# Tokens transposed while the modulation weights land, and the state-space heads with running sums kept as rows: one core, a hybrid block with mixture of experts

## The reference, cut to what matters

```python
mod_l = split((silu(c) @ w_ada + b_ada), 6); mod_c = split((silu(c_ctx) @ w_ada + b_ada), 6)
hl = rmsnorm(xl, norm1_g) * (1.0 + scale) + shift          # hc the same for the context
u = h @ w_in                                               # split in GLA | RWKV-7 | state space
...
# state space, 8 heads of 64, forward and backward, chunked
cum = cumsum(a);  decay = exp(where(causal, cum[:, None] - cum[None, :], -inf))
y = (einsum('tn,sn->ts', cm, bm) * decay) @ xdt  +  (cm * exp(cum)) @ s_start
...
kk = k * rw_kk; kk = kk * rsqrt(sum(kk * kk) + 1e-12); k = k * (1 + (a - 1) * rw_ka)
...
x = x + gate * (concat(o1, o2, rmsnorm(y * silu(z))) @ w_out)
x = x + gate2 * moe(rmsnorm(x, norm2_g) * (1 + scale2) + shift2)   # top 4 of 32 experts, d_ff 1024
return rmsnorm(x, final_norm_g)
```

## Time and profile before

| | us |
|---|---|
| median of 3 runs | 1395.98 (1394.66 to 1396.46) |
| profiled execution, span | 1395.1 |
| PE busy | 1289.9 (92%) |
| DVE busy | 377.9 (27%) |
| ACT busy | 250.8 (18%) |
| GpSimd busy | 48.9 (4%) |
| loaded from HBM | 451.8 MB, mean 325 GB/s |

### The profile page before, as it was taken

The page is one execution under the profiler, slowest core; times in us unless marked ns, Lnnn a source line. Parts: engine busy times, 40 slices in busy tenths (PEclk is TensorE's granted clock), DMA queues, the critical chain, the costliest instruction groups (busy, mean ns, idle before and its releaser), DMA issues.

```text
span 1395.1 us, 21339 instructions
## 1 busy us (share of the span) xinstructions
PE 1289.9 (92%) x9112; PEld 602.2 (43%) x9112; DVE 377.9 (27%) x910; ACT 250.8 (18%) x543; POOL 48.9 (4%) x81
## 2 busy tenths in 40 slices
PE   5999999968789999999999999999999999999997
PEld 2555466657678533333333333333333333333333
DVE  0214526855433221112111211121111211121112
ACT  2332212344331310101110111011100111011101
POOL 0002100051100000000000000000000000000000
PEclk9999999979989999999999999999999999999999
DMA  9464430130217699999999999999999999999994
GB/s 392 188 232 160 180 129 1 61 121 4 85 43 308 253 424 426 427 427 428 428 428 427 428 428 428 428 428 428 428 428 427 427 426 427 428 427 428 428 428 172
DMA packets 33482, 453.96 MB, mean 325 GB/s; under 512 B 3744, under 2 KB 4000, under 8 KB 4352
## 3 DMA queue, kind: packets, MB, share of 16 engines
q1 hardware_dynamic: 33408, 452.86, 77.4%
HBM read 451.79 MB, written 1.05 MB: 325 GB/s over the span
## 4 chain that ended last, share of the span: by engine, by line
PE 75%; DMA 12%; DVE 8%; ACT 2%; issue 2%; SPq 0%; DVEq 0%
PE PS L1823 72%; DMA arena<-in_moe_w_gu 10%; DMA arena<-in_ada_first 2%; PE PS L2591 1%; DVE arena L1717 1%; DVE arena L1241 1%; DVE arena L1723 1%; DVE arena L1720 1%; DMA arena<-in_ada_rest 1%; PE PS L2582 1%; DVE arena L1716 1%; PE PS L2241 0%; PE PS L1835 0%; DVE arena L1391 0%; DVE arena L1489 0%
## 5 line engine op out<-in xcount | busy, mean ns | idle before, releaser
L1823 PE MATMUL PS<-arena 128*64 128x512 f32 (+9 forms) x8762 | 1244.1, 425 | 62.1 <-DMA arena<-in_ada_first 15.5
L1823 PEld LDWEIGHTS PS<-arena 64*64 64x64 f32 (+5 forms) x8762 | 563.6, 149 | 688.9 <-issue 592.7
L1716 DVE TENSOR_SCALAR arena<-PS 128x256 f32<-128x256 f32 x64 | 38.6, 603 | 512.6 <-PE PS L1823 512.6
L1082 ACT ACTIVATE arena<-arena 128x256 f32<-128x256 f32 x64 | 26.7, 417 | 486.1 <-DVE arena L1716 486.1
L1745 DVE TENSOR_TENSOR arena<-PS,arena 128x512 f32<-128x512 f32 x32 | 22.1, 692 | 214.1 <-PE PS L1823 214.1
L1092 ACT COPY arena<-PS 128x256 f32<-128x256 f32 x32 | 11.9, 373 | 275.6 <-PE PS L2582 275.6
L2591 PE MATMUL PS<-arena 128*128 128x128 f32 x128 | 26.3, 287 | 32.2 <-DVE arena L1723 32.2
L1073 ACT ACTIVATE arena<-PS,arena 128x128 f32<-128x128 f32 x128 | 48.2, 457 | 36.9 <-PE PS L1823 36.9
L2591 PEld LDWEIGHTS PS<-arena 128*128 128x128 f32 x128 | 14.4, 142 | 58.5 <-DVE arena L1723 42.4
L1717 DVE TENSOR_SCALAR arena<-PS 128x256 f32<-128x256 f32 x64 | 39.2, 612 | 0.0
L1500 DVE COPY arena<-PS 128x384 f32<-128x384 f32 (+2 forms) x48 | 23.1, 488 | 56.4 <-PE PS L1823 56.2
(11 more groups left out here) (247 smaller groups left out, 371.1 us busy)
## 6 DMA issues: line engine op xcount, KB each, us to landing
arena<-in_moe_w_gu SPq DMA_DIRECT2D x128, 2048.0 KB, 25.4
arena<-in_moe_w_down SPq DMA_DIRECT2D x64, 2048.0 KB, 26.7
arena<-in_ada_rest SPq DMA_DIRECT2D x16, 1024.0 KB, 7.6
arena<-in_w_in SPq DMA_DIRECT2D x5, 2048.0 KB, 8.4
arena<-in_ada_first SPq DMA_DIRECT2D x4, 2048.0 KB, 14.4
arena<-in_w_out SPq DMA_DIRECT2D x4, 1024.0 KB, 5.8
arena<-in_tokens SPq DMA_DIRECT2D x1, 2048.0 KB, 20.9
arena<-in_consts SPq DMA_DIRECT2D x1, 1536.0 KB, 31.6
```

The costliest lines, as they stand in the source:

```text
L1082: act.activation(sgm[:, 256 * half:256 * half + 256], glu[:, 256 * half:256 * half + 256], ACT.Sigmoid, scale=ALPHA).then_inc(sig_ready, 1)
L1716: dve.tensor_scalar(by_rest(glu), of_half(0), LIMIT, None, ALU.min).then_inc(glu_ready, 1)
L1823: ins = pe.matmul(out, lhsT, rhs, start=start, stop=stop, skip_group_check=skip)
```

## The change

**Loads.** The tokens go ahead of the modulation weights; `mats` and the remaining constants go behind the first group of w_in and the next modulation block, and that block ahead of the second group.

**Opening.** The tokens are transposed and normalized between the modulation steps (after n = 1, 3 and 5). ScalarE and VectorE copy the pairs h0 to h3 out of PSUM as they are, into a buffer `raw` that lies over space used later. When shift and scale are there, both engines apply them from `raw` to `hT`, five k-blocks by VectorE and three by ScalarE, and the first projection waits for each block by itself. The time steps' matmuls go behind the second projection's first tile. There are fewer `stay_busy` matmuls.

**State-space heads.** The decays' logarithms are stored four times beside each other (`adt4`), so that four matmuls (`cs`) give the running sums of all sixteen as rows; ScalarE copies them to `sum_rows`, and `running_sums(q)` becomes four matmuls that spread a row over all partitions with a column of the identity, the two heads' in row groups 0 and 32, in turn. The time step is multiplied into the inputs by token (`xdt`, four VectorE operations out of PSUM) and not into the weights. Two of the six blocks of a head's weights need no clamp and are exponentiated by ScalarE straight from PSUM with a bias; VectorE clamps four blocks of 128, and multiplies all six with the scores in one operation. `WD` and `CI` hold four heads. `head_pair` alternates between the two heads. GpSimd's share of RWKV's inputs goes to VectorE. All three orders are rewritten.

```diff
+H_BY_VEC, H_BY_ACT = (0, 1, 3, 4, 6), (2, 5, 7)
...
-    t += [("Bt", 3, 1), ("sc", 0, 1), ("rk", 1, 1), ("cc", 3, 1), ("ada2", 4, 1), ("mt2", 4, 1), ("go", 3, 1), ("xst0", 2, 1), ("rr", 0, 1),
+    t += [("Bt", 3, 1), ("sc", 0, 1), ("rk", 1, 1), ("cc", 3, 1), ("cs", 3, 1), ("ada2", 4, 1), ("mt2", 4, 1), ("go", 3, 1), ("xst0", 2, 1), ("rr", 0, 1),
-    t += [("st", 1, 1), ("rv", 0, 1), ("rz0", 1, 1), ("rz1", 1, 1), ("ra", 1, 1), ("rkn", 0, 1), ("rg", 1, 1), ("rvt", 0, 1), ("cr", 1, 1)]
+    t += [("st", 1, 1), ("rv", 0, 1), ("rkn", 3, 1), ("rz0", 1, 1), ("rz1", 1, 1), ("ra", 1, 1), ("rg", 1, 1), ("rvt", 0, 1), ("cr", 1, 1)]
...
-            for n in (0, 2, 4):
+            sp.dma_start(xtok, a["tokens"]).then_inc(x_in, 16)
+            for n in (0, 2, 4, 6):
                 load_ada(n)
-            sp.dma_start(xtok, a["tokens"]).then_inc(x_in, 16)
-            load_ada(6)
...
+            for i in range(4):
+                R.arrived(act, f"h{i}")
+                R.drained(f"h{i}", act.copy(raw[:, 2 * i, :], pair(f"h{i}")[:, 0:NT]))
+            act.wait_ge(mod_ready, 1)
...
+            for k in H_BY_ACT:
+                for lo, hi, of in ((0, L, 1), (L, NT, 0)):
+                    ins = act.activation(hT[:, k, lo:hi], raw[:, k, lo:hi], ACT.Identity, bias=mod[:, k, of:of + 1], scale=A1[:, k, of:of + 1])
+                ins.then_inc(h_by_act, 1)
...
+            def head_exponents(q):
+                R.arrived(act, f"dc{q}")
+                if q >= 2:
+                    R.arrived(act, f"yp{q - 2}")
                 for hh in range(2):
+                    h, dc = 2 * q + hh, pair(f"dc{q}")[:, 512 * hh:512 * hh + 512]
+                    act.activation(WD[:, h % 4, F_OFF], dc[:, 128:256], ACT.Exp, bias=cumc[:, 2, h:h + 1])
+                    act.activation(WD[:, h % 4, B_OFF], dc[:, 256:384], ACT.Exp, bias=cumc[:, 3, 8 + h:9 + h])
+                    R.drained(f"dc{q}", act.activation(CI[:, h % 4], dc, ACT.Exp))
+                for hh in range(2):
+                    h = 2 * q + hh
+                    R.partly(act, f"dc{q}", 3 + hh)
+                    act.activation(WD[:, h % 4, F_2:F_OFF], WD[:, h % 4, F_2:F_OFF], ACT.Exp).then_inc(E_ready, 1)
...
+            for d in range(2):
+                for tt in range(2):
+                    ins = dve.tensor_tensor(xdt[d][:, tt, :].rearrange("p (h c) -> p h c", h=8),
+                                            pair("xst1")[:, 512 * tt:512 * tt + 512].rearrange("p (h c) -> p h c", h=8),
+                                            dtk[:, 2 + tt, 8 * d:8 * d + 8].unsqueeze(2).to_broadcast([P, 8, 64]), ALU.mult)
+            R.drained("xst1", ins)
...
             shift("rr", 0, (rT[:, 0, :], P, L), (rT[:, 1, :], P, L))
...
             shift("sg", 7, (sgT, 64, L))
...
+            clamps(0)
+            clamps(1)
+            weights(0)
+            decay_bias(0)
...
+            weights(1)
+            decay_bias(1)
+            gather_heads(0)
+            shift("rv", 4, (vT[:, 0, :], P, NT), (vT[:, 1, :], P, NT))
...
+            gather_heads(1)
...
+            clamps(2)
+            clamps(3)
+            weights(2)
+            weights(3)
+            gather_heads(2)
...
+            for n in range(8):
+                modulation(n)
+                if n == 1:
+                    pe.wait_ge(x_in, 16)
+                    pe.wait_ge(diag_ready, 4)
+                    normalized(0)
+                if n == 3:
+                    normalized(1)
+                    normalized(2)
+                if n == 5:
+                    normalized(3)
+                    stay_busy("dtp", 2 * BUSY_ADA)
+            modulation_columns(0)
+            stay_busy("dtp", BUSY_ADA)
...
             project_in("ll", 0)
             project_in("gq", 0)
+            time_steps()
             project_in("gq", 1)
...
+                for d in range(2):
+                    for hh in range(2):
+                        rows, col = slice(32 * hh, 32 * hh + 32), 32 * hh + 8 * d + 2 * q + hh
+                        at = 512 * hh + 256 * d
+                        ins = mm(pair(name)[:, at:at + 256], ident[rows, col:col + 1].to_broadcast([32, P]), sum_rows[rows, d, :])
...
```

More of the change, by code:

```diff
@@ L549, in hybrid_block @@
                         n_ada += 1
[L550 removed]
+        loads += [streamed(kind, n) for kind, n in (("in", 0), ("ada", 8), ("in", 1), ("ada", 9))]
         loads += [streamed(kind, n + 2) for kind, n in used if n + 2 < (len(W_GROUPS) if kind == "in" else 24)]
@@ new lines, in _ @@
+            head_exponents(0)
+            head_exponents(1)
+            R.emptied(act, "sg")
+            act.activation(sgT[0:64, :], sgT[0:64, :], ACT.Sigmoid).then_inc(gate_sig, 1)
+            R.emptied(act, "rz1")
+            act.activation(lw, lw, ACT.Sigmoid).then_inc(rz_sig, 1)
+            R.arrived(act, "ra")
+            for c in range(2):
+                ins = act.activation(ba[:, c, :], pair("ra")[:, 512 * c:512 * c + 512], ACT.Sigmoid,
+                                     bias=pc[:, 88 + 16 + c:88 + 17 + c])
+                if c == 0:
+                    step(ins)
@@ L951, in _ @@
-            R.drained("rvt", act.copy(Vt.rearrange("p a b -> p (a b)"), pair("rvt")))
+            head_exponents(3)
             def decays(s, d):
@@ L1202, in modulation @@
                 R.emptied(dve, f"mt{i}")
+            for i in range(4):
+                R.arrived(dve, f"h{i}")
+                R.drained(f"h{i}", dve.tensor_copy(raw[:, 2 * i + 1, :], pair(f"h{i}")[:, NT:2 * NT]))
             modulation_row(0)
@@ new lines, in clamps @@
+            def clamps(q):
+                for hh in range(2):
+                    h, dc = 2 * q + hh, pair(f"dc{q}")[:, 512 * hh:512 * hh + 512]
+                    R.partly(dve, f"dc{q}", 1 + 2 * hh)
+                    for i, (block, col) in enumerate(((F_2, cumc[:, 2, h:h + 1]), (F_3, cumc[:, 3, h:h + 1]),
+                                                      (B_2, cumc[:, 2, 8 + h:9 + h]), (B_3, cumc[:, 3, 8 + h:9 + h]))):
+                        ins = dve.tensor_scalar(WD[:, h % 4, block], dc[:, P * i:P * i + P], col, 0.0, ALU.add, ALU.min)
+                    R.drained(f"dc{q}", ins)
@@ new lines, in _ @@
+            gather_heads(1)
+            R.emptied(dve, "ra")
+            for c in range(2):
+                run(dve.tensor_scalar(ktmp[0][:, c, :], ba[:, c, :], -1.0, B(20 + c), ALU.add, ALU.mult))
+            run(dve.scalar_tensor_tensor(out=kT, in0=ktmp[0], scalar=1.0, in1=kT, op0=ALU.add, op1=ALU.mult))
+            clamps(2)
[3 more added lines that the diff above has]
+            gather_heads(2)
+            dve.wait_ge(kk_norm, 1)
+            run(dve.tensor_tensor(kk, kk, ktmp[1], ALU.mult))
@@ L1447, in _ @@
+            dve.tensor_tensor(ba, ba, kk, ALU.mult).then_inc(rw_pre, 1)
+            for c in range(2):
+                ins = dve.scalar_tensor_tensor(out=bon[:, c, :], in0=rT[:, c, :], scalar=B(22 + c), in1=kT[:, c, L:NT],
+                                               op0=ALU.mult, op1=ALU.mult)
+            ins.then_inc(rw_pre, 1)
             R.arrived(dve, "cr")
```

325 lines of the change are left out of this document (128 added, 197 removed).

## The result

The changed kernel runs in 1404.38 us (median of 8, 1403.04 to 1409.8) beside 1396.76 for the kernel before on the same chip: a ratio of 1.0043, 95% interval 1.0024 to 1.0062, some 6 us slower. The profiled execution (1408.04 us) lies 3.7 us over the median.

A forecast was written before the change was run, and what follows sets the result against it. DMA-bound experts form a fixed-length block from 500 us; instruction order sets its start. Terms -9.3 + 1.7 + 6.8 + 7.0 = +6.2 on 1395.1 give 1401.3; with 0.9 for the runs' median, 1402.2 us, range 1391 to 1408.

The forecast's parts named there:

- The opening: Start of the kernel: tokens first, first projection at 36.9 for 49.9 us, time-step sums moved later; gain 9.3 us.
- Sums as rows: State-space heads: four new matmuls and TensorE's wait for ScalarE's copy, hidden by nothing; +1.7 us.
- The third rival: Opening doesn't warm (+1.8) and row groups of the sums don't overlap (+2.6): 1406.6 us; chance 0.10.
- The reordered stretch and its clock: Heads up to the squares: new order adds waits, +6.8 us; half-rate TensorE clock at three places, +7.0 us.
- The addition: Durations summed along the new order from 223.9 us: squares' end at 307.3 against 300.5 at full clock, +6.8.
- its sign: What would show the forecast: the squares at 300.5 - 7.6 + 13.8 = 306.7 us.
- The second rival: Faster: clock holds and recurrences start warm, or VectorE's second-sums wait is under 6 us; 1392.5 us, chance 0.20.
- the first rival: The clock holds through the heads' waits, so the 7.0 us falls away: 1395.2 us, no change; chance 0.20.
- The stretch behind: After the squares, 305 to 312 us at 0.54 clock: starts as before, 0 us, ends -2.7 and +2.
- the warm start: Recurrences behind the squares begin with TensorE at full clock: another -2.7 us, part of the faster rival.
- The sum: Whole span: -9.3 + 1.7 + 6.8 + 7.0 = +6.2 us on 1395.1.
- GpSimd's products: Three products moved from GpSimd to VectorE before the last clamps: 3.9 us counted on VectorE's path.

The follow-up runs named there:

- m1_order: Changed kernel with VectorE's order edited: first pair's weights and the key norms' drain ahead of the second pair's clamps; ratio 0.9987 to the kernel before.
- o1_opening: Kernel before with only the change's opening (load order, raw copies, scaling from memory, moved time steps), old heads; ratio 0.9949 to the kernel before.
- b2_busy: Changed kernel with busy-work matmuls in six TensorE waits, in the second, smaller size; ratio 1.0007 to the kernel before.
- a2_after: Changed kernel run again unedited, as base and for a second profile; 1403.94 us, ratio 1.0042 to the kernel before.
- h1_heads: Changed kernel without its opening: row sums, alternating heads and new order behind the old opening; ratio 1.0086 to the kernel before.
- p1_pool: Changed kernel with three products (new keys, normalized keys, their product with a) back on GpSimd; ratio 1.0011 to the kernel before.
- b0_busy: Kernel before with 30 calls of busy work in its 7.42 us TensorE wait ahead of the router row; ratio 0.9976 to the kernel before.
- m3_pool: Changed kernel with all engines' order written anew, plus three products back on GpSimd; 1379.52 us, ratio 0.9846 to the kernel before.
- m2_order: Changed kernel with one order written anew for three engines, no operation added or removed; 1378.72 us, ratio 0.984 to the kernel before.
- s1_sums: Changed kernel with the running sums in their old form, eight matmuls per pair; ratio 1.0045 to the kernel before.
- s2_sums: Changed kernel with the order written anew and the running sums in their old form; ratio 0.9867 to the kernel before.

## Why the prediction was right, and where it wasn't

**The opening** (9.3): first projection at 37.48 for 36.9, own share at the copy 8.7. The mechanism is right, the size slightly over.

**Sums as rows** (1.7): 2.0 by the copies of m1_order and o1_opening, which have no dip ahead of it. Row groups do overlap: a pair's sums took 1.13 us at the full clock in b2_busy (1.0 forecast, 1.75 without overlap, 2.72 before). The third rival's two conditions both failed (its 2.6 us has no working).

**The reordered stretch and its clock** (6.8 + 7.0 = 13.8): 14.4 in after's and a2_after's profiles, 10.5 in h1_heads' with the same code, so that 14.4 comes so near to 13.8 is in part luck. The waits are where the sum had them: 9.29 for 9.7 before the second clamps, 8.78 for 9 before the first pair, 3.45 for 3.8 at the first sums; the other "4 us" before the states was 1.68, since the gate's projection ran at the half rate in its place. The addition is 0.3 us too high by slips in its partial sums (253.4 and not 253.2 ahead of VectorE's wait, to begin with), and its sign, the squares at 306.7, was missed by 3.2 us, which is the 3.4 us of the dip ahead of the copy that no term held. m1_order gives 8.1 us back by order with as much half rate as after; b2_busy gives 4.9 with VectorE's wait as it was, of which h1_heads' scatter of 3.9 can be a part. So the order is shown as a cause with its size, the clock as a cause with its size open; that the two add up was not tried.

**The second rival** named a VectorE wait under 6 us, or dips under 3.4 us in all with warm recurrences, and the first a clock that holds. There was a wait of 9.29 us, there were four dips, and the clock was 0.50 again from 310 us on. Both fell in this profile. b2_busy, which comes nearer to the first rival's clock, is at 1.0007, no change, as that rival said (1395.2).

**The stretch behind** (0, -2.7 to +2) is the term that was mis-sized. After's +1.7 is inside. Over the thirteen profiles beside before's it went from -2.6 (h1_heads) to +7.8 us (a2_after) against before, mean +2.5, with the same code. Most of it arises in the recurrences and the output projection: from the squares to the router's first MAX8 a2_after took 169.2 us with 27.3 of them at the half rate, before 161.2 with 17.1, and h1_heads 160.6 with 10.2. So 6.7 of the opening's 10.2 us were gone at the end of o1_opening's profile, and 7.1 is what its runs keep (5.1 by the medians). The bounds should have been set by such scatter, and the warm start played no part that the runs show.

**The sum** (+6.2) came within 2 us of the medians (+6.0 by the ratio, +7.6 by the runs): -8.7 + 2.0 + 14.4 = +7.7, and 1.7 behind, is 9.4; the two dips ahead of the copy (3.4 in this execution, 1.7 no longer lost from before) bring it to the +11.1 of this profile's span, which is the slow side of the kernel's scatter.

**GpSimd's products** stood in the sum on VectorE's path. They were on it in part: without 4.7 us of them p1_pool came 2.9 us sooner from the drain of rv to the squares.

## What to carry to other kernels

An instruction that waits for the second round (here the second pair's clamps), put ahead of a drain that the other engine needs to go on with the first, costs what that engine has to do in between: before rewriting three orders, write for each drain what is queued ahead of it. Work saved on TensorE need not be time saved where TensorE waits: here the same operations gave +6 us in one order and -22 us in another. And a profile of one execution carries several us of the clock's scatter, so a term is read between two marks and not from the span, and in more than one profile: the same code took 98.3, 98.3 and 94.3 us between them.

## What was not expected of the hardware

The granted clock fell to 0.50 at 194 us while TensorE was never idle. What stood in front of it, in after from 191.95 to 194, and in before from 200.4 to 203.2, where its own fall follows (line, operation, shapes, count, busy us and mean ns, idle):

```profile
L1830 PE MATMUL PS<-arena 128*128 128x8 f32 x19 | 2.3, 260 | 0.0
L1823 PE MATMUL PS<-arena 128*128 128x8 f32 x24 | 2.8, 257 | 0.0
```

These are matmuls of 8 columns, the sums of the decays' logarithms by token (`cc`). The three profiles with the old opening (before, h1_heads, b0_busy) show the fall at 202.5 to 203.2, also without a wait ahead of it. Of the eleven with the new opening seven show it at 193 to 195; o1_opening, m1_order, p1_pool and m3_pool have none, though a2_after and m2_order run the same code to there. s1_sums and s2_sums show it without row sums, so it isn't their doing. What decides in an execution stays open. The Trainium skill (TensorE: Matmul & The Clock Gate, HAM oscillation) ties the lower clock to waits between bursts; here there was no wait, so the trace shows a case beside the rule. The same page (What's actually happening) says that the count of slow matmuls at a kernel's start varies from run to run; the profiles here show such a variation in the middle of one.
